# Layer 0's second branch: queries with keys, and values with gates, projected at once, in units of four contraction blocks by 512 columns

## The chip, the core and the metric

The kernel runs on one core of a Trainium2 chip. A time is the device time of one execution in microseconds (us); less is better. The time of a kernel is the median of several runs. Beside that there is one profiled execution, whose span and rows are quoted below. Engines are called TensorE (PE), VectorE (DVE), ScalarE (ACT), GpSimd (POOL) and SyncE (SP), which issues the weight loads.

## What is computed

Two blocks of two layers each run over 512 tokens (256 of a context and 256 of the sequence) with a model width of 1024. The change lies in the first layer of the first block, in its second branch: differential attention over 8 heads, each with two maps of width 64 and values of width 128.

```
bq, bk, bv, bz = columns of h @ w_in            # 1024 columns each, h is 512 x 1024
qh = rmsnorm(bq.reshape(n, 8, 2, 64), q_norm_w)  # over the 64
kh = rmsnorm(bk.reshape(n, 8, 2, 64), k_norm_w)
if not context: qh, kh = apply_axial_rope(qh, rope), apply_axial_rope(kh, rope)
s = q @ k.T / 8;  p = softmax(s);  w = p[map 0] - lam * p[map 1]
y_b = rmsnorm(w @ v) * (1 - lam_init) * silu(bz)
```

Context tokens attend to the context (256 keys), the other tokens to all 512. All is float32.

## The kernel before

**Projections.** Weights come from memory in units of 1 MB (128 partitions by 2048 words), through a ring of two buffers `raw`. ScalarE writes the high part of a unit, rounded to the fp32r type of the matmul, to `wh` (`used`, `convert`, L1750 and L1751: 1280 and then 768 words), and VectorE the rest, `raw - wh`, to `wl` (L2528 and L2530, or L2548 from `used_part`). There are two buffers of each as well, so a unit can be converted as soon as TensorE is through with the unit two places before it. The activations `H` are in two parts too. A product is three matmuls (`mm3`): high by high, high by low, low by high.

**The branch.** `branch_b` exists once for each engine, and each engine runs its own list in order. Heads are taken in four pairs. For layer 0 a pair has 16 slots, one for each kind (q, k, v, z) and token tile of 128 tokens, in the order q0 to q3, k0 to k3, v0 to v3, z0 to z3. In a slot `proj_k` does the projection of a tile onto the pair's 256 columns of the kind: 8 contraction blocks by 3 matmuls of 256 columns, with the tile of `H` stationary. A kind's weights are one unit. Two tiles share a PSUM bank; q, v and z use banks 0 and 1, k banks 7 and 6.

`chunk_b` takes the results in the slot after: for q and k ScalarE squares two tiles from PSUM into `b_qn`, VectorE sums the squares, and after the second pair of tiles it computes one reciprocal root for the kind (`root`, eight small operations and one to add eps) and multiplies PSUM by it into `b_qn`. GpSimd then weights the context tiles (0 and 1) and rotates the others (four half-width products with tables `wtab`, L3468, and an addition). In slots 13 and 15 TensorE transposes the pair's queries and keys into banks 6 and 7, and ScalarE copies them to `b_qt`. v is copied and z goes through tanh on ScalarE; VectorE completes the gate.

**The attention of a pair** runs beside the projections of the next one, planned by `slot_b`. A pair has 8 items j (two heads by four query tiles). Scores of an item are in slot 15, 17, 19, ... (every second slot), its transposes two slots later and its product with the values three slots later. Between them lie, on VectorE, the maximum and its factor (L2887, L2513), on ScalarE two exponentials (TMG<-PS), on VectorE the shares (L2875 and then L2517, writing colS, colC and TMG), which TensorE's transpose waits for. TensorE does not start an item's scores before the exponentials of the item before it are done. VectorE does the shares in the slot after the scores. Four items make an output: factors and products by the gate on VectorE (`b_done_slot`), four transposes on TensorE into bank 6 (`b_out_slot`), copies on ScalarE and VectorE into `YB`.

In VectorE's list a slot is: shares, maximum, output, results of the projection (`chunk_b`), conversion of a unit, factors. The first branch's values (`values_of`) are already projected in half units, four contraction blocks by 512 columns, as are those of the Fourier branch (`pair`).

Of the kernel before, what the change touches and what calls it, by code (L numbers as in the profile page):

```python
# [33 lines left out]
def plan_units():  # L34
# [34 lines left out]
    for l in range(2):  # L69
# [21 lines left out]
        for p in range(4):  # L91
# [130 lines left out]
def program(nc, wpk, xin, memt, vec, tabs, tabs2, rpb, out):  # L222
# [13 lines left out]
    with ctx:  # L236
# [217 lines left out]

        def b_chunk(l, n):
# [177 lines left out]
        def tensor_program(P):  # L633
# [354 lines left out]
            def merge_b(l):  # L988
# [29 lines left out]
                for j in range(8):  # L1018
# [4 lines left out]
                    elif l == 0:  # L1023
                        P.wait_ge(dve_step, ("b_z", l, 3, j))
# [22 lines left out]
            def slot_b(l, n):  # L1047
# [28 lines left out]
                if pj := B_VALUES[l].get(n):  # L1076
                    a, t_, nk = b_tile(l, pj[1])
                    P.wait_ge(act_step, ("b_wt", l, *pj))
                    P.wait_ge(act_step, ("b_v", l, pj[0], 1))
# [6 lines left out]
                    t.then_inc(*pe_step.mark(("b_pv", l, *pj)))  # L1086

            def branch_b(l):
# [18 lines left out]
                for n in range(B_BASE[l]):  # L1107
                    p, kind, t_ = b_chunk(l, n)
                    i, half = divmod(t_, 2)
                    slot_b(l, n)  # L1110
                    if (a := B_QK[l].get(n % B_PER[l])) is not None:
                        for c, x in enumerate("qk"):
# [5 lines left out]
                            free[6 + c] = act_step, ("b_qk", l, p, a)  # L1118
                    b = b_bank(l, kind, i)
                    if half == 0:  # L1120
# [3 lines left out]
                        elif kind == "q":  # L1124
                            if p:
                                P.wait_ge(*((dve_step, ("b_z", l, p - 1, i)) if l == 0 else (act_step, ("b_v", l, p - 1, 1))))
                            else:
                                P.wait_ge(act_step, ("m_gate", l, "a", 6 + b))
                        elif kind == "v":
                            if l == 0 or i:  # L1130
# [5 lines left out]
                        else:  # L1136
                            P.wait_ge(act_step, ("b_v", l, p, i if l == 0 else 0))
                    u = place["b_" + kind, 4 * l + p]
# [599 lines left out]
        def scalar_program(A):  # L1738
# [266 lines left out]
            def merge_b(l):  # L2005
# [13 lines left out]
                used("b_z", 4 * l + 3)  # L2019
# [10 lines left out]
            def slot_b(l, n, chunk=None):  # L2030
# [14 lines left out]
                if chunk is not None:  # L2045
                    chunk_b(l, chunk)
# [10 lines left out]
                if pj := B_VALUES[l].get(n):  # L2057
# [8 lines left out]
                    act(y, bank(5)[:, 128 * i:128 * i + 128], ACT.Copy, ("b_osq", l, *pj))  # L2066

# [24 lines left out]
            def branch_b(l):  # L2092
                t0, N = lay(l)
                for n in range(B_BASE[l]):
                    slot_b(l, n, n - 1 if n else None)
# [8 lines left out]
                    if n and b_chunk(l, n - 1)[2] == 3 and (b_chunk(l, n - 1)[1] != "q" or l == 0):  # L2104
                        used("b_" + b_chunk(l, n - 1)[1], 4 * l + n // B_PER[l] - (n % B_PER[l] == 0))
                    if l and n % B_PER[l] == 4:
                        used("b_q", 4 * l + n // B_PER[l])
# [399 lines left out]
        def vector_program(D):  # L2507
# [327 lines left out]
            def merge_b(l):  # L2835
# [14 lines left out]
                slot_b(l, base, base - 1, ("b_z", 4 * l + 3))  # L2850
# [16 lines left out]
            def slot_b(l, n, chunk=None, unit=()):  # L2867
# [22 lines left out]
                if pg := B_OUT[l].get(n):  # L2890
# [3 lines left out]
                        YB[0][:, heads_, t0:512], ALU.mult, ALU.subtract, *events)  # L2894
                if chunk is not None:
                    chunk_b(l, chunk)
# [4 lines left out]
                if pg := B_DONE[l].get(n):  # L2901
# [5 lines left out]
                    for i in range(4):  # L2907
                        a, t_, nk = b_tile(l, 4 * g + i)
                        stt(b_yt[k][:, i], b_yt[k][:, i], small[:, 40 + i:41 + i], b_z[p % 2][:, t_, a], ALU.mult, ALU.mult, ("b_yo", l, p, g))

# [24 lines left out]
            def branch_b(l):  # L2935
# [9 lines left out]
                for n in range(1, B_BASE[l]):  # L2945
                    p, kind, t_ = b_chunk(l, n - 1)
                    slot_b(l, n, n - 1, ("b_" + kind, 4 * l + p) if t_ == 3 and kind != "q" else ())
                    if l and n % B_PER[l] == 4:
                        used("b_q", 4 * l + p)
                    if l == 0 and n % B_PER[l] in (5, 6):  # L2950
                        used_part("b_q", p, n % B_PER[l] - 5)
# [514 lines left out]
        def pool_program(G):  # L3466
# [24 lines left out]
            def branch_b(l):  # L3491
# [14 lines left out]
                for n in range(1, B_BASE[l] + 1):  # L3506
                    p, kind, t_ = b_chunk(l, n - 1)
                    if kind in "qk" and t_ == 3:
                        c = "qk".index(kind)
                        ones = lambda x, m: x.unsqueeze(1).to_broadcast([128, m, 64])  # L3510
                        if kind == "k" or l == 0:
                            G.wait_ge(dve_step, ("b_norm", l, p, kind, 0))
                            x = b_qn[c][:, 0:2].rearrange("p t (g d) -> p (t g) d", d=64)
                            tt(x, x, ones(b_w[:, c], 8), ALU.mult)
                        G.wait_ge(dve_step, ("b_norm", l, p, kind, 1))
                        G.wait_own(pool_step)
                        for t in range(2):
                            x = b_qn[c][:, 2 + t].rearrange("p (g s d) -> p g s d", g=4, s=2)
                            m2 = b_m2[:, t].rearrange("p (g s d) -> p g s d", g=4, s=2)
                            sines = b_tab[:, c, 1, t].rearrange("p (s d) -> p s d", s=2).unsqueeze(1).to_broadcast([128, 4, 2, 32])  # L3520
                            tt(m2, x[:, :, ::-1], sines, ALU.mult)
                        G.wait_own(pool_step)
                        for t in range(2):
                            x = b_qn[c][:, 2 + t].rearrange("p (g d) -> p g d", d=64)
                            tt(x, x, ones(b_tab[:, c, 0, t], 4), ALU.mult)
                        G.wait_own(pool_step)
# [362 lines left out]
```

## Time and profile before

| | us |
|---|---|
| median of 3 runs | 2238.47 |
| lowest and highest | 2237.56, 2239.45 |
| the profiled execution | 2240.27 |
| its span | 2238.1 |

The span runs from the first to the last instruction in the profile. Busy time is counted per engine and overlaps between engines. Matmuls are pipelined, so their durations overlap one another: what a stream of them costs is read from the distance of their starts, not from their durations. A row `xN` merges N instructions of one kind that follow one another. In the timeline the text in square brackets is the idle time before a row and what ended it.

### The profile page before, as it was taken

How to read it: one execution, taken by the hardware profiler on the slowest of the kernel's cores; microseconds unless marked ns; L12 is line 12 of the kernel's file. 1: busy time of each engine (PE TensorE's matmuls, PEld its weight loads, DVE VectorE, ACT ScalarE, POOL GpSimd, SP SyncE). 2: the span in 40 equal slices, each digit the busy share in tenths (PEclk: the TensorE clock that was granted, in tenths of full speed). 3: DMA queues.
4: the chain of work that ended last, by engine and by line, in shares of the span. 5: the costliest groups of instructions: out<-in, count | busy, mean ns of one | idle time of the engine just before them, and what ended most of it. 6: DMA issues, size and time to landing. Idle time of an engine off the chain costs nothing.

```text
span 2238.1 us, 34826 instructions
## 1 busy us (share of the span) xinstructions
PE 2215.1 (99%) x14398; PEld 1948.8 (87%) x14398; DVE 1350.9 (60%) x2589; ACT 1046.2 (47%) x1994; POOL 273.4 (12%) x298
## 2 busy tenths in 40 slices
PE   8999999999999999999999999999999999999998
PEld 7888878999978888878899999999888888988887
DVE  6644523566755243466465776557777776667875
ACT  5543422345442233354443455445466554466553
POOL 0000000222201032100002220120210110120110
PEclk9999999999999999999999999999999999999999
DMA  8522134221224222235343223446533545324544
GB/s 313 186 94 78 74 151 171 76 77 58 76 97 148 94 76 94 85 132 170 113 151 132 76 95 114 170 170 211 158 110 147 188 169 187 133 95 151 188 173 147
DMA packets 55534, 298.07 MB, mean 133 GB/s; under 512 B 9344, under 2 KB 16256, under 8 KB 24208
## 3 DMA queue, kind: packets, MB, share of 16 engines
q1 hardware_dynamic: 53040, 291.62, 36.4%
q10 hardware_dynamic: 2336, 4.23, 0.8%
q8 instruction: 113, 1.85, 0.3%
q14 instruction: 45, 0.37, 0.1%
HBM read 292.65 MB, written 3.44 MB: 132 GB/s over the span
## 4 chain that ended last, share of the span: by engine, by line
PE 92%; DVE 5%; ACT 2%; DMA 1%; issue 0%; ACTq 0%; POOL 0%; SPq 0%; DVEq 0%
PE PS L637 88%; PE PS L641 4%; DVE TM L2509 1%; ACT TM L1740 1%; DVE wl L2528 1%; ACT TMG L1740 0%; DVE wl L2530 0%; DMA raw<-in_wpk 0%; DVE colS L2517 0%; DMA Y<-factors_d 0%; DVE HY L2517 0%; DVE TM L2678 0%; DVE TMG L2517 0%; ACT wh L1750 0%; ACT HY L1740 0%
## 5 line engine op out<-in xcount | busy, mean ns | idle before, releaser
L637 PE MATMUL PS<-HY,wh 128*128 128x512 f32 (+3 forms) x4944 | 1282.4, 343 | 5.1 <-ACT TM L1740 1.4
L637 PEld LDWEIGHTS PS<-HY,wh 128*128 128x128 f32 (+2 forms) x4944 | 847.9, 189 | 121.5 <-issue 8.5
L637 PE MATMUL PS<-HY,wl 128*128 128x256 f32 (+1 forms) x3000 | 925.0, 308 | 0.0
L637 PEld LDWEIGHTS PS<-HY,wl 128*128 128x128 f32 x3000 | 566.7, 189 | 30.0
L2528 DVE TENSOR_TENSOR wl<-raw,wh 128x1280 fp32r<-128x1280 f32 (+1 forms) x238 | 346.9, 1458 | 387.8 <-ACT wh L1750 387.7
L637 PE MATMUL PS<-wh,HY 128*128 128x256 f32 (+1 forms) x2468 | 527.3, 306 | 0.2
L1740 ACT ACTIVATE TM<-PS 128x512 f32<-128x512 f32 (+3 forms) x399 | 196.7, 508 | 527.9 <-PE PS L637 417.9
L637 PEld LDWEIGHTS PS<-wh,HY 128*128 128x128 f32 x2468 | 405.9, 191 | 19.7 <-ACT TM L1740 0.8
L1750 ACT ACTIVATE wh<-raw 128x1280 fp32r<-128x1280 f32 (+2 forms) x246 | 295.7, 1202 | 245.4 <-PE PS L637 163.5
L637 PE MATMUL PS<-wl,HY 128*128 128x256 f32 (+1 forms) x1234 | 373.4, 303 | 0.0
L2530 DVE TENSOR_TENSOR wl<-raw,wh 128x768 fp32r<-128x768 f32 (+1 forms) x238 | 248.8, 1045 | 0.0
L637 PEld LDWEIGHTS PS<-wl,HY 128*128 128x128 f32 x1234 | 236.1, 191 | 8.6
L1751 ACT ACTIVATE wh<-raw 128x768 fp32r<-128x768 f32 (+2 forms) x246 | 200.2, 814 | 0.0
L637 PE MATMUL PS<-TM 64*128 64x512 f32 (+5 forms) x704 | 134.0, 396 | 1.9 <-ACT TM L1740 1.1
L3468 POOL TENSOR_TENSOR HY<-TM,HY 128x256 fp32r<-128x256 f32 (+2 forms) x64 | 62.7, 980 | 351.2 <-ACT HY L1740 350.2
L1740 ACT ACTIVATE TMG<-PS 128x512 f32<-128x512 f32 (+2 forms) x121 | 51.5, 444 | 105.2 <-PE PS L637 98.0
L637 PEld LDWEIGHTS PS<-TM 64*128 64x128 f32 (+2 forms) x704 | 80.4, 189 | 18.0 <-issue 7.4
L2509 DVE TENSOR_TENSOR TM<-PS,TM 128x512 f32<-128x512 f32 (+3 forms) x92 | 47.7, 547 | 72.4 <-ACT TM L1740 70.2
L1740 ACT ACTIVATE TMG<-PS,colS 128x512 f32<-128x512 f32 (+1 forms) x108 | 63.8, 598 | 54.3 <-DVE colS L2513 54.1
L3468 POOL TENSOR_TENSOR TM<-TM,wtab 128x256 f32<-128x256 f32 x64 | 68.2, 1085 | 75.6 <-DVE colS L2875 69.1
L3468 POOL TENSOR_TENSOR TM<-TM,T 128x512 f32<-128x512 f32 (+2 forms) x30 | 31.0, 1048 | 373.9 <-PE PS L637 189.2
L1740 ACT ACTIVATE HY<-TM 128x256 fp32r<-128x256 f32 (+2 forms) x82 | 42.0, 519 | 60.4 <-POOL TM L3468 31.6
(195 smaller groups left out, 1701.9 us busy)
## 6 DMA issues: line engine op xcount, KB each, us to landing
raw<-in_wpk SPq DMA_DIRECT2D x233, 1024.0 KB, 4.8
raw<-in_wpk SPq DMA_DIRECT2D x32, 704.0 KB, 4.1
TM<-in_wpk SPq DMA_DIRECT2D x6, 1024.0 KB, 16.6
Y<-factors_d ACTq DMA_DIRECT2D x16, 256.0 KB, 5.0
X<-in_xin SPq DMA_DIRECT2D x1, 2048.0 KB, 15.4
Y<-in_wpk SPq DMA_DIRECT2D x2, 1024.0 KB, 20.3
Y<-bias_d SPq DMA_DIRECT2D x4, 512.0 KB, 10.2
raw<-in_wpk SPq DMA_DIRECT2D x3, 512.0 KB, 3.6
```

Of the source, the lines that this page charges most:

```text
L637: return P.x.matmul(o, l, r, start=start, stop=stop)
L641: return P.x.transpose(o, i, ident[0:p, 0:p])
L1740: return A.x.activation(o, i, f, **kw).then_inc(*act_step.mark(*events))
L1750: A.x.activation(wh[:, s, 0:c], raw[:, r, 0:c], ACT.Copy).then_inc(*hi_split.mark((u, 0)))
L1751: A.x.activation(wh[:, s, c:n], raw[:, r, c:n], ACT.Copy).then_inc(*hi_split.mark((u, 1)))
L2509: return D.x.tensor_tensor(o, a, b, op).then_inc(*dve_step.mark(*events))
L2528: D.x.tensor_tensor(wl[:, s, 0:c], raw[:, r, 0:c], wh[:, s, 0:c], ALU.subtract).then_inc(*lo_split.mark((u, 0)))
L2530: D.x.tensor_tensor(wl[:, s, c:n], raw[:, r, c:n], wh[:, s, c:n], ALU.subtract).then_inc(*lo_split.mark(u))
L3468: return G.x.tensor_tensor(o, a, b, op).then_inc(*pool_step.mark(*events))
```

## The change

For layer 0 only, a pair's four units are now two of queries with keys and two of values with gates. Each holds four of the eight contraction blocks, and 256 columns of either kind. The number of units, their size and their places in the list of loads stay.

```diff
+        for p in range(4) if l == 0 else ():
+            qk = [base + 256 * p + 64 * i + d for base in (4112, 5136) for i in range(4) for d in halves]
+            for k0 in (0, 4):
+                add("b_qk", [("w_in", l, qk)], k0=k0, kn=4)
+            for k0 in (0, 4):
+                add("b_vz", [("w_in", l, r(base + 256 * p, base + 256 * p + 256)) for base in (6160, 7184)], k0=k0, kn=4)
```

A slot is a tile and a half of the contraction: 4 blocks by 3 matmuls of 512 columns. The order of the 16 slots, the slots in which a unit ends, and the banks:

```diff
+        B_PARTS = ([("qk", 0, t) for t in (0, 1, 2, 3)] + [("qk", 1, t) for t in (2, 3, 0, 1)]
+                   + [("vz", half, t) for pair in (0, 2) for half in range(2) for t in (pair, pair + 1)])
+        B_UNIT_ENDS = {3: ("b_qk", 0), 7: ("b_qk", 1), 13: ("b_vz", 0), 15: ("b_vz", 1)}
+        b_squares = T[:, 908:1420]
+        def b_part_bank(kind, t):
+            if kind == "qk":
+                return (6, 7, 0, 1)[t]
+            return t % 2
-            return b_value_slot(l, p, 4 * g + 3) + ((8, 4), (3,))[l][g]
+            if l == 0:
+                return b_value_slot(l, p, 4 * g + 3) + (4, 10 if p < 2 else 4)[g]
+            return b_value_slot(l, p, 3) + 3
```

The last lines are `b_out_slot`: the output transposes move from slots 0 and 4 to slots 12 and 10. A tile of q and k now fills a bank. Its results, taken after slots 5 and 7 for two tiles at a time, go another way. ScalarE:

```diff
+            def part_b(n):
...
+                    act(squares_, src[0], ACT.Square, ("b_sq", 0, p, "q", i), scale=0.125)
+                    for c in range(2):
+                        act(dst[c], src[c], ACT.Copy, ("b_copy", 0, p, c, i))
+                    A.wait_own(act_step)
+                    A.wait_ge(dve_step, ("b_sum", 0, p, i, "q"))
+                    act(squares_, dst[1], ACT.Square, ("b_sq", 0, p, "k", i), scale=0.125)
...
+                    act(b_v[p % 2][:, t].rearrange("p a d -> p (a d)"), bank(b)[:, 0:256], ACT.Copy, ("b_v", 0, p, t))
...
+                    act(b_z[p % 2][:, t].rearrange("p a d -> p (a d)"), bank(b)[:, 256:512], ACT.Tanh, ("b_zt", 0, p, t), scale=0.5)
```

VectorE, with one root for both kinds of two tiles, and products from SBUF to SBUF:

```diff
+            def part_b(n):
...
+                    for c, x in enumerate("qk"):
+                        D.wait_ge(act_step, ("b_sq", 0, p, x, i))
+                        D.x.reduce_sum(ss[:, 8 * c:8 * c + 8], wide(b_squares), AX).then_inc(*dve_step.mark(("b_sum", 0, p, i, x)))
+                    root(colS[:, 0:16], colS[:, 16:32], ss, eps=EPS)
+                    D.wait_own(dve_step)
+                    for c, x in enumerate("qk"):
+                        D.wait_ge(act_step, ("b_copy", 0, p, c, i))
+                        y = wide(b_qn[c][:, 2 * i:2 * i + 2].rearrange("p t d -> p (t d)"))
+                        tt(y, y, colS[:, 8 * c:8 * c + 8].unsqueeze(2).to_broadcast([128, 8, 64]), ALU.mult, ("b_norm", 0, p, x, i))
+                if half and kind == "vz":
+                    zt = b_z[p % 2][:, t].rearrange("p a d -> p (a d)")
+                    D.wait_ge(act_step, ("b_zt", 0, p, t))
+                    stt(zt, zt, 1.0, bank(b_part_bank(kind, t))[:, 256:512], ALU.add, ALU.mult, ("b_z", 0, p, t))
```

Where a unit is converted (ScalarE; in VectorE's slot 8 the conversion goes ahead of the results as well):

```diff
+                    ends = b_unit_end(n - 1) if n and l == 0 else None
+                    if ends and n % 16 in (8, 14):
+                        used(*ends)
                     slot_b(l, n, n - 1 if n else None)
...
+                    if ends and n % 16 not in (8, 14):
+                        used(*ends)
```

TensorE, a part of a tile:

```diff
+            def part(p, kind, half, t, end):
+                u, b = place["b_" + kind, 2 * p + half], b_part_bank(kind, t)
+                w, v = weights(u)
...
+                for k in range(4):
+                    split_done(u, k)
+                    P.wait_ge(*h_ready(0)(4 * half + k))
+                    own = slice(128 * t, 128 * t + 128)
+                    x = mm3(bank(b), H[0][:, 4 * half + k, own], H[1][:, 4 * half + k, own], w[:, k], v[:, k],
+                            half == 0 and k == 0, half == 1 and k == 3)
```

GpSimd: the tiles that are rotated (2 and 3) are ready first, so the order of a pair is now rotation of q, rotation of k, weighting of q, weighting of k, where it was weighting and rotation of q, then weighting and rotation of k:

```diff
+                for p in range(4):
+                    if l == 0:
+                        rotated(p, "q")
+                        rotated(p, "k")
+                        weighted(p, "q", ("b_ready", l, p, "q", 1))
+                        weighted(p, "k", ("b_ready", l, p, "k", 1))
+                        continue
```

## Rows read from the trace of the kernel before

**Rows 1.** The page: TensorE's busy time; the chain that ended last, by engine and line.
```profile
PE 2215.1 (99%) x14398; PEld 1948.8 (87%) x14398; DVE 1350.9 (60%) x2589; ACT 1046.2 (47%) x1994; POOL 273.4 (12%) x298
...
PE 92%; DVE 5%; ACT 2%; DMA 1%; issue 0%; ACTq 0%; POOL 0%; SPq 0%; DVEq 0%
PE PS L637 88%; PE PS L641 4%; DVE TM L2509 1%; ACT TM L1740 1%; DVE wl L2528 1%; ACT TMG L1740 0%; DVE wl L2530 0%; DMA raw<-in_wpk 0%; DVE colS L2517 0%; DMA Y<-factors_d 0%; DVE HY L2517 0%; DVE TM L2678 0%; DVE TMG L2517 0%; ACT wh L1750 0%; ACT HY L1740 0%
```

**Rows 2.** Windows of the first and last pair: length, each engine's busy us, clock, DMA.
```profile
379.20:427.50 48.30, 48.30 (x402) 47.83 (x402) 22.73 (x44) 14.96 (x23) 17.35 (x24) 1.00 0.35 125
...
555.54:620.25 64.71, 64.58 (x515) 59.09 (x514) 45.96 (x112) 32.87 (x86) 15.06 (x12) 1.00 0.18 66
```

**Rows 3.** Chain in order of time, slots 8 to 11, third pair: start, us, what.
```profile
522.86 0.61 ACT TM L1740
...
526.09 1.29 DVE TM L2509 x2
527.38 2.11 DVE wl L2528
...
531.74 1.03 ACT TMG L1740 x4
...
534.96 0.44 PE PS L641 x2
```

**Rows 4.** Timeline of TensorE, third pair: start, us, line, operands, shape, count.
```profile
522.65 1.05 PE L637 MATMUL PS<-TM 128*128 128x128 f32 x8
...
527.90 0.28 PE L637 MATMUL PS<-wl,HY 128*128 128x256 f32 x1
...
528.26 0.28 PE L637 MATMUL PS<-wl,HY 128*128 128x256 f32 x1
...
533.71 1.13 PE L637 MATMUL PS<-TM 64*128 64x512 f32 x4
```

**Rows 5.** Timeline of TensorE in the first branch's values.
```profile
190.40 0.39 PE L637 MATMUL PS<-wl,HY 128*128 128x512 f32 x1
...
191.08 0.39 PE L637 MATMUL PS<-wl,HY 128*128 128x512 f32 x1
```

**Rows 6.** Groups by line and form, 379 to 621 us: count, busy us, mean ns.
```profile
L637 PE MATMUL PS<-wh,HY 128*128 128x256 f32 x1024 | 196.1, 287 | 0.0
```

**Rows 7.** Timeline of TensorE in the Fourier branch.
```profile
734.47 0.39 PE L637 MATMUL PS<-wl,HY 128*128 128x512 f32 x1
...
735.17 0.39 PE L637 MATMUL PS<-wl,HY 128*128 128x512 f32 x1
```

**Rows 8.** The page, parts 5 and 6: high part of a unit on ScalarE; weight loads.
```profile
L1750 ACT ACTIVATE wh<-raw 128x1280 fp32r<-128x1280 f32 (+2 forms) x246 | 295.7, 1202 | 245.4 <-PE PS L637 163.5
...
raw<-in_wpk SPq DMA_DIRECT2D x233, 1024.0 KB, 4.8
```

**Rows 9.** Timeline of VectorE, slots 5, 6 and 8 to 10 of the third pair.
```profile
513.61 0.53 DVE L2513 TENSOR_SCALAR colS<-colS 128x2 f32<-128x2 f32 x1
514.05 1.48 DVE L2548 TENSOR_TENSOR wl<-raw,wh 128x1280 fp32r<-128x1280 f32 x1
...
527.29 2.20 DVE L2528 TENSOR_TENSOR wl<-raw,wh 128x1280 fp32r<-128x1280 f32 x1
...
530.83 0.68 DVE L2887 TENSOR_REDUCE colS<-PS 128x2 f32<-128x512 f32 x1
531.54 0.17 DVE L2513 TENSOR_SCALAR colS<-colS 128x2 f32<-128x2 f32 x1
...
533.13 1.25 DVE L2517 SCALAR_TENSOR_TENSOR colC<-colS 128x1 f32<-128x1 f32 x1
```

**Rows 10.** Timeline of GpSimd: third pair of layer 0; one row of layer 1.
```profile
526.86 1.28 POOL L3468 TENSOR_TENSOR TM<-TM,T 128x512 f32<-128x512 f32 x1 [6.79 <-DVE TM L2509]
528.29 4.73 POOL L3468 TENSOR_TENSOR TM<-TM,wtab 128x256 f32<-128x256 f32 x4
533.09 1.28 POOL L3468 TENSOR_TENSOR TM<-TM 128x512 f32<-128x512 f32 x1
...
1233.86 3.28 POOL L3468 TENSOR_TENSOR TM<-TM,wtab 128x256 f32<-128x256 f32 x4 [20.18 <-DVE colS L2875]
```

More of the change, by code:

```diff
@@ L90, in plan_units @@
         merge("a", 10256)
-        for p in range(4):
+        for p in range(4) if l == 0 else ():
[4 more added lines that the diff above has]
+                add("b_vz", [("w_in", l, r(base + 256 * p, base + 256 * p + 256)) for base in (6160, 7184)], k0=k0, kn=4)
+        for p in range(4) if l else ():
             for tag, base in (("b_q", 4112), ("b_k", 5136)):
@@ L1086, in slot_b @@
                     t.then_inc(*pe_step.mark(("b_pv", l, *pj)))
+            def part(p, kind, half, t, end):
+                u, b = place["b_" + kind, 2 * p + half], b_part_bank(kind, t)
+                w, v = weights(u)
+                if half == 0 and kind == "qk":
+                    if b >= 6:
+                        P.wait_ge(*free[b])
+                        free[b] = act_step, ("b_copy", 0, p, 1, 0)
+                    elif p:
+                        P.wait_ge(dve_step, ("b_z", 0, p - 1, t))
+                    else:
+                        P.wait_ge(act_step, ("m_gate", 0, "a", 6 + b))
+                elif half == 0:
+                    P.wait_ge(*((dve_step, ("b_z", 0, p, t - 2)) if t >= 2 else (act_step, ("b_copy", 0, p, 1, 1))))
+                for k in range(4):
[4 more added lines that the diff above has]
+                            half == 0 and k == 0, half == 1 and k == 3)
+                if half or end:
+                    x.then_inc(*projected.mark(*([("b_" + kind, 0, p, t)] if half else []), *([("unit", u)] if end else [])))
             def branch_b(l):
@@ L1107, in branch_b @@
                 for n in range(B_BASE[l]):
-                    p, kind, t_ = b_chunk(l, n)
-                    i, half = divmod(t_, 2)
+                    if l:
+                        p, kind, t_ = b_chunk(l, n)
+                        i, half = divmod(t_, 2)
+                    else:
+                        p, kind, half, t_ = b_part(n)
                     slot_b(l, n)
@@ L1118, in branch_b @@
                             free[6 + c] = act_step, ("b_qk", l, p, a)
+                    if l == 0:
+                        part(p, kind, half, t_, b_unit_end(n))
+                        continue
                     b = b_bank(l, kind, i)
@@ L1136, in branch_b @@
                         else:
[L1137 to L1138 removed]
+                            P.wait_ge(act_step, ("b_v", l, p, 0))
+                    u = place["b_" + kind, p]
                     proj_k(bank(b)[:, 256 * half:256 * half + 256], u, H, h_ready(l), 8, 128 * t_, ("b_" + kind, l, p, t_),
@@ L2894, in slot_b @@
                         YB[0][:, heads_, t0:512], ALU.mult, ALU.subtract, *events)
+                if unit and l == 0 and n % 16 == 8:
+                    used(*unit)
+                    unit = ()
                 if chunk is not None:
-                    chunk_b(l, chunk)
+                    chunk_b(l, chunk) if l else part_b(chunk)
                 if pj and b_turn_slot(l, *pj) == n + 1:
@@ L3505, in branch_b @@
                         tt(b_tab[:, c, 1, t, 32:64], b_cs[:, 1, t, 32:64], w[:, 0:32], ALU.mult)
[L3506 to L3526, printed above, removed]
-                        tt(b_qn[c][:, 2:4], b_qn[c][:, 2:4], b_m2, ALU.add, ("b_ready", l, p, kind, 1))
```

98 lines of the change are left out of this document (83 added, 15 removed).

## The prediction, made before the changed kernel had run

> **What bounds the kernel now.** The page comes first: TensorE is busy 99% of the span, and 92% of the chain that ended last lies on it, 88% on one line [rows 1]. So the change gains what it takes from TensorE's stream and loses what TensorE has to wait for. [...] The chain in order of time shows where the stage is tight even now: it leaves TensorE at 522.86, runs over the keys' norm, the conversion of a weight unit, the maximum of the next scores, the exponential and the shares on VectorE, and comes back to TensorE's transpose only at 534.96 [rows 3]. I therefore follow this place slot by slot. A slot is one of the 16 pieces of projection work in a pair; slot 8 of this pair (the third) begins at 522.65 and its slot 11 at 533.71 [rows 4].
>
> **What the matmuls give.** A slot's projection is 24 matmuls of 256 columns now and 12 of 512 columns then. Three matmuls (high by high, high by low, low by high) start 0.36 us apart as groups of 256 columns [rows 4], so a slot costs 8 x 0.36 = 2.88 us. Groups of 512 columns start 0.68 us apart in the first branch's values, which have the same operand roles [rows 5]: 4 x 0.68 = 2.72 us. The branch has 1024 such matmuls with the high part of the weights [rows 6] and, by the code, half as many with the low part, 1536 in all, that is 64 slots. Gain: 64 x 0.16 = **10.2 us**. The bound on the other side is the Fourier branch, where groups of 512 start 0.70 us apart [rows 7]; its stationary operand takes every other column, the new code takes neighbouring ones, so I take 0.68. At 0.70 the gain would be 64 x 0.08 = 5.1 us. Attention matmuls, transposes and their number stay.
>
> **Edits that cost nothing by themselves.** DMAs: the same 16 units of 1 MB in the same queue, with the small bias transfers after the same places in order; a unit's load is issued after the conversion two units earlier, and that leaves at least five slots, some 17 us, against a landing of 4.8 us [rows 8]. ScalarE gets four copies, two SBUF squares and eight narrow evacuations in place of wide ones, about 3 us more per pair (0.61 us for 512 elements [rows 3]), and has 31.8 us idle in a pair. One root for both kinds and two token tiles, twice a pair, is as many root steps as before. Two units of values and gates are now open together, so three conversions have four slots or two slots of time: two slots are 5.4 us of projection and 6.5 to 8 us with attention, ScalarE needs 1.2 us for the larger part of a conversion [rows 8] and, by its 768 words, 0.8 for the smaller, VectorE 1.5 [rows 9] and 0.9; from its start it is some 3.8 us until VectorE is through. That is hidden, provided both engines are free. The output transposes only change their slots (0.44 us each).
>
> **What becomes late: the slot 8 chain.** VectorE works in order: in slot 8 it does the last shares, the conversion, then the whole norm of token tiles 0 and 1 for queries and keys, and only then the maximum of slot 9's scores. TensorE's next scores, in slot 11, wait for that exponential. Now, from the start of slot 8: square until 0.8 and sum until 1.5, root until 3.4 (so it takes 1.9), the two norms of 1.29 together until 4.7, the conversion until 8.2, maximum and exponential until 10.15 [rows 3, 9]; slot 11 begins at 11.06. Margin 0.9 us, for an exponential that ends at 532.77 and scores that start at 533.71. After the change:
> - Slot 6 now has a full chain as well (square q, sum, square k, sum, root, two norms, where it had one square and one sum). It starts behind slot 5's exponential and holds VectorE until about 3.5 us into slot 7. So slot 7's exponential ends 1.6 us after the start of slot 8 instead of 1.1 before it.
> - ScalarE's conversion follows it: high part at 2.9, low parts 1.5 + 0.9 until 5.2.
> - Sum q 0.7, square k 0.6, sum k 0.7 (a sum of 512 elements as the maximum of 512, 0.68 [rows 9], the square as the 0.61 of [rows 3]): 7.1. Root and norms 3.2: 10.3. Maximum, factor and exponential 2.0 [rows 9]: 12.3.
> - Slot 11 begins at 11.0 (three slots shorter by 0.16, an output transpose in slot 10 longer).
> So TensorE is 1.2 to 1.4 us late without any contention; with a small wait for a late transposed copy, or for the shifted output in slot 12 (its factors are ready about 0.3 to 0.4 late), I take 1.5 us a pair, for the three pairs that have attention beside them.
>
> **Contention of VectorE with GpSimd.** This is the larger term. While GpSimd has an operation running, VectorE's operations on SBUF operands last longer: the larger part of a conversion 2.20 us against 1.48, a two-element factor 0.53 against 0.17, and an operation on a single column 1.25 [rows 9]; the 2.20 and the 1.25 began 0.43 and 0.04 us after a GpSimd operation and got through once it had ended (526.86 + 1.28, 533.09 + 1.28) [rows 10]. GpSimd suffers in turn: its four half-width products take 4.73 us beside conversions and 3.28 us without them [rows 10]. So the operations take turns, whole ones at a time. [...]
>
> In the old order GpSimd did keys' rotation alone after slot 8. In the new one it starts at the end of slot 6's norm and does two rotations on end, 2 x (3.3 + 1.3), then both weightings, 2 x 1.4, and the norms themselves now read and write SBUF (they read PSUM). I interleave them by turns: shares of slot 7's scores lose about 0.8 us to the last products of q; the conversion waits for one addition and one product, 1.6 us more; the root meets the keys' addition, 1.3; the two-element factor meets a weighting, 0.7. That is 4.4 us on the same chain. The exponential comes 5.6 us late where each turn is lost, of which 2.1 us is already taken in slot 10 (the transposed copy is behind the late square on ScalarE). The old trace lost about 1.3 us there in a comparable spot, and turns aren't always lost: 0 is the lower bound, 4.4 the upper, and I take 3.7, near the upper because VectorE's six us of such work fall into a stretch in which GpSimd is almost never idle. Per pair 1.5 + 3.7 = 5.2 us, three pairs: **15.6 us**.
>
> **The first pair.** No attention, slots of 2.72. Norm of slot 6 is done 22.1 us after the branch's start, GpSimd needs 2 x 6.1 + 2 x 1.4 = 15.0 us by its rows with conversions beside it [rows 10] and ends at 37.1; the transposes of slot 13 want it at 35.4 and 35.9. So 1.3 us, 2.7 if the root's small steps also take turns with it; I take **2.3 us**.
>
> **Sum.** -10.2 + 15.6 + 2.3 = +7.7 us. Against the profiled execution, 2240.27 us with a span of 2238.1, that is 2248.0. That execution stands 1.8 us above the median of the runs, 2238.47, and carrying the change to the median gives 2246.2. I forecast **2246**, slower. What a measurement can tell from no change is 0.2%, 4.5 us: 2234.0 to 2242.9.
>
> **Rivals.**
> - *Chains late, little lost in turns.* Gain 10.2, loss 3 x 1.5 + 1.3 = 5.8: 2234.1; with half the turns lost, 3 x 2.2 = 6.6 more: 2240.7. For it: what reads PSUM does not lengthen (the maximum at 530.83 takes 0.68 us with GpSimd at work beside it [rows 9, 10]), so part of the chain is immune. Against: the rows of conversions. Mostly within 0.2%.
> - *All hidden, the gain stands.* This is the other side: if TensorE's matmul stream is the only thing that counts and VectorE catches up before slot 11, 2238.5 - 10.2 = 2228.3. It decides from a slot 8 chain 1.3 us shorter than I reckon, with no turn lost. For it: VectorE's 18.7 idle us in the last pair [rows 2]. Against: the margin of 0.9 us now, with one norm less in front of it.
> - *More is late.* All turns lost and a second place behind it (the factors of slot 12, or slot 13's scores): some 8 us a pair, 3 x 8 + 2.7 - 10.2 = +16.5: 2255. Or 512 columns at 0.70: +5.1 on the forecast, 2251.
> - *The columns don't matter.* If groups of 512 took as long as two of 256 (0.72), the gain is 0 and only the delays remain, 2256. The rows of the first branch speak against it.
>
> **Numbers.** Forecast case (2243 to 2251) 0.46; little lost 0.31; all hidden 0.13; more late, with the columns, 0.10. Of the second case 0.04 lies below 2234.0 and 0.02 above 2242.9. Faster 0.04 + 0.13 = 0.17, same 0.25, slower 0.02 + 0.46 + 0.10 = 0.58. The range of 8 in 10 is 2233 to 2253: it leaves out the hidden case and the worst of the last.
>
> **What would show it.** Right: 768 projection matmuls of 512 columns in groups 0.68 apart; idle time of TensorE in slots 10 and 11 of pairs 2 to 4, released by ScalarE's exponential or transposed copy; the last of the chain over colC, colS and wl on VectorE, pairs longer than 64.7 us by 2 to 3; some wait for GpSimd in the first pair's slot 13; conversions of slot 8 longer than 1.5 us. Wrong: pairs of 62 us with TensorE never idle (turns and chains hidden), or idle time released by DMA or by an unfinished conversion, which I price at nothing.

## The result, and the profile after

The changed kernel takes 2260.22 us (median of 4 runs, 2258.51 to 2262.21), the kernel before beside it 2238.56: 1.0097 times as long, with a 95% interval of 1.0084 to 1.011. The prediction had 2246 and a range that ended at 2253: the direction was right, the size was not. The profiled execution took 2262.21 us, with a span of 2260.1.

The page after: TensorE has 768 matmul records fewer than in [rows 1] and the same busy time. Its part of the chain that ended last fell from 92% to 88%, and VectorE's rose to 7%.

```profile
PE 2215.4 (98%) x13630; PEld 1909.8 (84%) x13630; DVE 1356.2 (60%) x2597; ACT 1057.2 (47%) x2026; POOL 267.3 (12%) x298
...
PE 88%; DVE 7%; ACT 3%; DMA 1%; issue 1%; ACTq 0%; POOL 0%; SPq 0%; DVEq 0%
```

The windows of the branch after (from and to, length, busy us and instructions of TensorE, its weight loads, VectorE, ScalarE and GpSimd, granted clock as a share of full speed, DMA share, GB/s). In [rows 2] TensorE covered the first pair (48.3 us) and the last (64.7 us) at a clock of 1.00. Now it is busy for 2.13 of the 8 us from 380 us on, and there and at 420 us the mean clock falls. In windows of 2 us it is 0.50 from 384 to 388 us, 0.53 to 390 and 1.00 from there on; behind the second wait it is 0.50 from 424 to 426 us, 0.65 to 428 and then 1.00. By "the lower level" the 0.50 is meant. The pairs 2 to 4 take 67.2 to 68.3 us.

```profile
380.00:388.00 8.00, 2.13 (x5) 1.75 (x6) 2.95 (x5) 2.00 (x2) 2.04 (x9) 0.69 0.63 245
388.00:396.00 8.00, 8.00 (x32) 6.46 (x32) 0.00 (x0) 0.00 (x0) 0.81 (x4) 0.88 0.17 69
...
420.00:428.00 8.00, 5.56 (x20) 4.12 (x19) 3.30 (x7) 0.66 (x2) 4.07 (x3) 0.79 0.00 0
438.00:505.20 67.20, 63.46 (x311) 47.58 (x310) 43.01 (x101) 34.40 (x90) 13.38 (x12) 0.97 0.21 72
505.20:573.20 68.00, 64.63 (x321) 48.72 (x320) 46.30 (x114) 35.63 (x94) 13.32 (x12) 0.97 0.18 62
573.20:641.50 68.30, 64.77 (x321) 48.52 (x320) 46.23 (x114) 35.62 (x94) 13.37 (x12) 0.98 0.18 62
```

TensorE's timeline after has eight waits over 0.3 us in the branch; the kernel before had none between 379 and 648 us. These are the first four (start, us, line, operation, and in brackets the idle time and what ended it); the third and fourth pair repeat the last two with 0.51 and 2.85, 1.31 and 2.22 us. Behind the first two the next groups of 512 columns start 1.28 us apart (386.46 and 387.74, 424.29 and 425.57), and scores that took 1.13 us in [rows 4] take 2.08.

```profile
385.87 0.79 PE L673 MATMUL PS<-wh,HY 128*128 128x512 f32 x1 [6.59 <-DVE T L2626]
386.46 0.63 PE L673 MATMUL PS<-wl,HY 128*128 128x512 f32 x1
...
387.74 0.63 PE L673 MATMUL PS<-wl,HY 128*128 128x512 f32 x1
...
423.13 0.50 PE L673 MATMUL PS<-wh,HY 128*128 128x512 f32 x1 [2.44 <-DVE TM L2623]
...
424.29 0.63 PE L673 MATMUL PS<-wl,HY 128*128 128x512 f32 x1
...
425.57 0.63 PE L673 MATMUL PS<-wl,HY 128*128 128x512 f32 x1
...
476.53 0.71 PE L673 MATMUL PS<-TM 128*128 128x128 f32 x4 [1.49 <-ACT TM L1805]
...
482.23 2.08 PE L673 MATMUL PS<-TM 64*128 64x512 f32 x4 [2.26 <-ACT TMG L1805]
```

The first wait read back, in the chain in order of time (start, us, what): the load of a weight unit, its conversion on ScalarE and VectorE, and behind that in VectorE's queue the copy of the rotary and weight tables out of bank 6. Slot 0 now writes to bank 6. In the kernel before it wrote to bank 0, and the same copy at 385.12 us held up nobody: slot 0 had begun at 379.21.

```profile
376.82 4.71 DMA raw<-in_wpk
...
381.56 1.28 ACT wh L1815
...
382.86 1.49 DVE wl L2634
384.35 0.87 DVE wl L2636
...
385.28 0.54 DVE T L2626 x2
...
385.87 10.34 PE PS L673 x36
```

The two rows of the kernel before, slot 0's first matmul and the copy:

```profile
379.21 0.39 PE L637 MATMUL PS<-wh,HY 128*128 128x256 f32 x1
...
385.12 0.61 DVE L2520 COPY T<-PS 128x256 f32<-128x256 f32 x2
```

### The profile page after: what moved, and what is told of

The parts are those of the page before. It is cut to its first block, busy times and chain, and to the rows that moved or that the text cites. A ratio compares the mean times of both kernels' runs of the same rounds, so it can differ in the third digit from the quotient of the medians.

```text
span 2260.1 us, 33356 instructions
## 1 busy us (share of the span) xinstructions
PE 2215.4 (98%) x13630; PEld 1909.8 (84%) x13630; DVE 1356.2 (60%) x2597; ACT 1057.2 (47%) x2026; POOL 267.3 (12%) x298
## 3 DMA queue, kind: packets, MB, share of 16 engines
q10 hardware_dynamic: 2336, 4.23, 0.8%
## 4 chain that ended last, share of the span: by engine, by line
PE 88%; DVE 7%; ACT 3%; DMA 1%; issue 1%; ACTq 0%; POOL 0%; SPq 0%; DVEq 0%
PE PS L673 85%; PE PS L677 3%; DVE TM L2615 1%; DVE wl L2634 1%; ACT TMG L1805 1%; ACT TM L1805 1%; DVE colS L2623 1%; DVE wl L2636 1%; DMA raw<-in_wpk 1%; ACT wh L1815 0%; DVE TMG L2623 0%; DVE colC L3029 0%; DVE colS L2993 0%; DMA Y<-factors_d 0%; DVE HY L2623 0%
## 5 line engine op out<-in xcount | busy, mean ns | idle before, releaser
L2634 DVE TENSOR_TENSOR wl<-raw,wh 128x1280 fp32r<-128x1280 f32 (+1 forms) x242 | 351.6, 1453 | 412.6 <-ACT wh L1815 412.4
L673 PE MATMUL PS<-wh,HY 128*128 128x256 f32 (+1 forms) x1956 | 506.8, 343 | 9.2 <-DVE T L2626 6.6
L673 PEld LDWEIGHTS PS<-wh,HY 128*128 128x128 f32 x1956 | 342.0, 192 | 49.4 <-DVE T L2626 6.7
L673 PE MATMUL PS<-wl,HY 128*128 128x256 f32 (+1 forms) x978 | 330.6, 338 | 0.0
L2636 DVE TENSOR_TENSOR wl<-raw,wh 128x768 fp32r<-128x768 f32 (+1 forms) x242 | 254.9, 1053 | 0.0
L673 PEld LDWEIGHTS PS<-wl,HY 128*128 128x128 f32 x978 | 187.5, 192 | 17.6
L3599 POOL TENSOR_TENSOR TM<-TM,wtab 128x256 f32<-128x256 f32 x64 | 62.8, 1002 | 240.8 <-DVE TM L2615 169.0
L2615 DVE TENSOR_TENSOR TM<-TM 128x256 f32<-128x256 f32 (+7 forms) x146 | 65.7, 465 | 6.2 <-POOL TM L3599 1.3
```

What stands on the lines that cost most here:

```text
L673: return P.x.matmul(o, l, r, start=start, stop=stop)
L2615: return D.x.tensor_tensor(o, a, b, op).then_inc(*dve_step.mark(*events))
L2634: D.x.tensor_tensor(wl[:, s, 0:c], raw[:, r, 0:c], wh[:, s, 0:c], ALU.subtract).then_inc(*lo_split.mark((u, 0)))
L2636: D.x.tensor_tensor(wl[:, s, c:n], raw[:, r, c:n], wh[:, s, c:n], ALU.subtract).then_inc(*lo_split.mark(u))
L3599: return G.x.tensor_tensor(o, a, b, op).then_inc(*pool_step.mark(*events))
```

## The measure used below: how far the scores are behind

An attention item's scores are the same matmuls in all kernels, in every second slot. The start of such a matmul, less its start in the kernel before, tells how much a kernel has lost up to there. Two rows of the kernel before, of slots 9 and 13 of the second pair,

```profile
461.81 0.70 PE L637 MATMUL PS<-TM 64*128 64x256 f32 x4
...
476.81 1.13 PE L637 MATMUL PS<-TM 64*128 64x512 f32 x4
```

and those of the changed kernel:

```profile
471.23 0.70 PE L673 MATMUL PS<-TM 64*128 64x256 f32 x4
...
491.57 1.13 PE L673 MATMUL PS<-TM 64*128 64x512 f32 x4
```

Differences of this kind, in us (s9 is slot 9 of a pair; "end" is the first slot behind the fourth pair; the columns are the kernels e1, e7, e2, e12, e8 and e4 of the next section):

| scores, start before | changed | tables moved | wait added to before | GpSimd out | both: tables, GpSimd | idle filled | chain in slot 9 |
|---|---|---|---|---|---|---|---|
| pair 1 s15, 423.46 | 10.55 | 2.06 | 9.53 | 6.24 | -2.44 | 7.08 | 10.15 |
| pair 2 s9, 461.81 | 9.42 | 0.92 | 9.53 | 5.11 | -3.57 | 5.94 | 9.01 |
| pair 2 s13, 476.81 | 14.76 | 5.51 | 9.54 | 6.57 | -2.12 | 10.57 | 14.85 |
| pair 3 s9, 526.51 | 12.54 | 3.29 | 9.53 | 4.35 | -4.34 | 8.35 | 12.64 |
| pair 3 s13, 541.51 | 18.08 | 8.76 | 9.54 | 6.45 | -2.23 | 13.70 | 17.36 |
| pair 4 s9, 591.21 | 15.86 | 6.54 | 9.53 | 4.23 | -4.45 | 11.48 | 15.14 |
| pair 4 s13, 606.21 | 21.58 | 12.22 | 9.54 | 6.62 | -2.05 | 17.03 | 20.05 |
| end, 620.77 | 20.76 | 11.40 | 9.54 | 5.81 | -2.87 | 16.25 | 19.24 |

One thing in these differences is neither gain nor loss. An output's four transposes take TensorE 0.43 us, and five outputs stood between a slot 13 and the next slot 9 (or the end) and stand between slots 9 and 13 now. So 5 x 0.43 = 2.2 us of work has moved from the one kind of stretch to the other. A row of the kernel before, in slot 0 of the third pair; the next transposes start at 491.28:

```profile
490.85 0.60 PE L641 MATMUL PS<-T,TM 128*128 128x128 f32 x4
```

## Experiments

Unless said otherwise an edit is made to the changed kernel (2260.22 us). Every ratio is to the kernel before, run beside it on the same chip. `...` in an edit stands for lines left out.

**The tables in another bank** (e1_tables).

```diff
-  mm(bank(6)[:, 128 * c + 64 * t_:...], rope1[0:64, c, ...
+  mm(bank(4)[:, 128 * c + 64 * t_:...], rope1[0:64, c, ...
-  free[6] = dve_step, ("b_tables", l)
+  if l:
+      free[6] = dve_step, ("b_tables", l)
...
-  cp(b_cs.rearrange("p s t d -> p (s t d)"), bank(6)[:, 0:256])
+  cp(b_cs.rearrange("p s t d -> p (s t d)"), bank(4)[:, 0:256])
...
```

> Layer 0's rotary and weight tables go to bank 4 and no longer to bank 6, so slot 0 of the second branch no longer waits for VectorE's copy of them. Theory (the start wait is a loss of its own, which the prediction missed): the wait of 6.59 us ahead of the first matmul of slot 0 goes, and with it most of the stretch in which the next groups start 1.28 us apart; the time falls by 6.6 + 2 to about 2251.5 us. Rival (the wait is only handed on: the weights of slot 0 or 1, or the banks of slots 2 and 3, which the late conversions hold up as well, are waited for next): the idle time of TensorE between 379 and 396 us stays within 2 us of 6.6, and the time stays at 2258 to 2261.

Measured: 2249.28 us, ratio 1.0043 (1.0027 to 1.0058). The wait is gone and nothing took its place: in the windows from 372 to 396 us TensorE is busy throughout, at a clock of 1.00. By the scores the start was worth 10.55 - 2.06 = 8.5 us, 6.6 of them idle; in the pairs 2 to 4 the kernel then loses nearly what the changed one loses (15.7 us from slot 9 to slot 13 in sum, against 16.6). The medians differ by 10.9 us, of which the branch has 20.76 - 11.40 = 9.4. The theory holds.

**The same wait in the kernel before** (e7_before_wait).

```diff
+ if l == 0:
+     P.wait_ge(dve_step, ("b_tables", l))
  for n in range(B_BASE[l]):
```

> The kernel before with one wait more: TensorE waits for VectorE's copy of layer 0's tables ahead of the first matmul of the second branch, as slot 0 of the changed kernel does. Theory (the wait alone makes the loss at the start, whatever the units' shape): TensorE is idle for some 6.5 us from 379.2, the groups after it run at the lower clock for some us, and the time rises by 8 to 11 us to 2247 to 2250. Rival (before, work later in the pair has slack that takes the wait up, or the clock stays): 2244 or less.

Measured: 2249.84 us, 1.0043 (1.0028 to 1.0058), 9.3 us more than before. TensorE is idle for 6.85 us, the windows behind show a clock of 0.62 and 0.74, and the scores are 9.53 us late at once and stay exactly that late to the end of the branch. So the wait makes this loss with the old units as well, and no slack later on takes it back.

```profile
380.00:388.00 8.00, 1.97 (x9) 1.97 (x10) 2.95 (x5) 2.00 (x2) 1.87 (x8) 0.62 0.59 230
388.00:396.00 8.00, 8.00 (x53) 8.00 (x53) 0.58 (x1) 0.60 (x1) 0.97 (x5) 0.74 0.21 84
396.00:412.00 16.00, 16.00 (x136) 16.00 (x135) 7.24 (x16) 3.09 (x4) 7.14 (x6) 1.00 0.12 44
```

**GpSimd's part left out** (e2_no_gpsimd).

```diff
- rotated(p, "q"); rotated(p, "k"); weighted(p, "q", ...); weighted(p, "k", ...)
...
+ tt(b_qn[c][:, 0, 0:1], b_qn[c][:, 0, 0:1], b_w[:, c, 0:1], ALU.mult, ("b_ready", l, p, x, 1))
```

> GpSimd's rotation and weighting of layer 0's queries and keys is left out but for one element each, so what follows computes with unrotated values. [...] Rival (the order alone: the norm chain put ahead of the results of the slot): the waits stay at 3 us or more a pair and the time stays above 2255.

Measured: 2247.78 us, 1.0039 (1.0026 to 1.0052), where 2244 us was the forecast if the turns with GpSimd make a good part of the loss. The wait at slot 12 of the first pair is gone, and those of the pairs 2 to 4 sum to 1.31, 1.35 and 1.64 us. VectorE's timeline shows why. The root in the changed kernel, first pair, beside GpSimd (GpSimd's rows there: 416.81 for 2.98 us, 419.86 for 1.31), and the shares and the conversion of the second pair:

```profile
416.76 0.17 DVE L2619 TENSOR_SCALAR small<-colC 128x16 f32<-128x16 f32 x1
416.97 0.60 DVE L2620 TENSOR_SCALAR colS<-small 128x16 int32<-128x16 int32 x1
417.61 0.66 DVE L2615 TENSOR_TENSOR colS<-colS 128x16 f32<-128x16 f32 x1
...
420.06 1.35 DVE L2623 SCALAR_TENSOR_TENSOR colS<-colS 128x16 f32<-128x16 f32 x2
...
469.43 1.54 DVE L2623 SCALAR_TENSOR_TENSOR TMG<-TMG,colS 128x256 f32<-128x256 f32 x1
470.89 2.02 DVE L2634 TENSOR_TENSOR wl<-raw,wh 128x1280 fp32r<-128x1280 f32 x1
472.83 1.49 DVE L2636 TENSOR_TENSOR wl<-raw,wh 128x768 fp32r<-128x768 f32 x1
```

and the same instructions without GpSimd:

```profile
415.94 0.17 DVE L2619 TENSOR_SCALAR small<-colC 128x16 f32<-128x16 f32 x1
416.15 0.17 DVE L2620 TENSOR_SCALAR colS<-small 128x16 int32<-128x16 int32 x1
416.36 0.17 DVE L2615 TENSOR_TENSOR colS<-colS 128x16 f32<-128x16 f32 x1
...
417.40 0.39 DVE L2623 SCALAR_TENSOR_TENSOR colS<-colS 128x16 f32<-128x16 f32 x2
...
464.60 0.49 DVE L2623 SCALAR_TENSOR_TENSOR TMG<-TMG,colS 128x256 f32<-128x256 f32 x1
465.24 1.49 DVE L2634 TENSOR_TENSOR wl<-raw,wh 128x1280 fp32r<-128x1280 f32 x1 [0.15 <-ACT wh L1815]
466.64 0.95 DVE L2636 TENSOR_TENSOR wl<-raw,wh 128x768 fp32r<-128x768 f32 x1
```

The four products of GpSimd's row at 416.81 end at 417.55, 418.24, 419.09 and 419.78, and the four root steps that take 0.60 to 0.67 us there end at 417.57, 418.27, 419.12 and 419.82. That, and the 0.17 us of each without GpSimd, is what "turns" stands for.

**Its control, and both cures together** (e11_before_no_gpsimd: the same left out of the kernel before; e12_tables_no_gpsimd: e1's and e2's edits together).

> The control: the kernel before with GpSimd's rotation and weighting of layer 0's queries and keys left out but for one element each (what follows computes with unrotated values). In the kernel before TensorE had no wait over 0.3 us between 379 and 648 us, so by the theory (GpSimd's turns cost time only where VectorE's queue has no slack) nothing comes of it: 2236 to 2240 us. Rival (GpSimd's work costs the second branch time in either kernel, so the gain of the changed kernel without it says nothing about the change): 2232 or less.

> The changed kernel with the tables in bank 4 and without GpSimd's rotation and weighting of layer 0 (the same part left out). Theory: the start's loss (9.5 to 11 us) and the turns' loss (12.4 us alone, the wait at slot 12 with it) stand by themselves, so 2260.2 - 11 - 12.4 = 2237 us; against the control the columns' gain of 10 to 11 us less what VectorE's order alone costs in the pairs 2 to 4 (6 us by the offsets of the scores' starts) leaves -4 us or so. Rival (the two losses share a part): 2240 or more.

Measured: the control 2238.7 us, 1.0 (0.999 to 1.0009): GpSimd's turns cost the kernel before next to nothing (0.59 us at the end of the branch). Both cures 2237.67 us, 0.9992 (0.9982 to 1.0001), where the sum of the two gave 2237: the losses stand by themselves. Against the control that is only 1.0 us less, not 4; the scores at the end of the branch say 2.3 less (-2.87 against -0.59).

The kernel with both cures shows the columns' gain and the order's price without the other terms. In the first pair the groups of 512 columns start 0.68 us apart; in the pairs 2 to 4, with attention between them, 0.69. A slot's projection lasts 2.82 to 2.95 us there until the next operation starts, and 2.95 to 3.05 in the kernel before, where groups of 256 are 0.36 apart throughout. Two rows of the third pair, one group apart:

```profile
493.24 0.39 PE L673 MATMUL PS<-wl,HY 128*128 128x512 f32 x1
...
493.93 0.39 PE L673 MATMUL PS<-wl,HY 128*128 128x512 f32 x1
```

TensorE waits 4.3 us in sum in the pairs 2 to 4: 1.9 for the exponential (slot 11), 0.8 for the factored outputs and 1.6 for the gate of the first tile (both slot 12). The third pair:

```profile
530.02 1.13 PE L673 MATMUL PS<-TM 64*128 64x512 f32 x4 [0.39 <-ACT TMG L1806]
...
534.68 0.66 PE L677 MATMUL PS<-T,TM 128*128 128x128 f32 x4 [0.41 <-DVE TM L2624]
...
536.34 0.50 PE L673 MATMUL PS<-wh,HY 128*128 128x512 f32 x1 [0.56 <-DVE TM L2624]
```

**Idle time filled** (e3_keep, e8_keep_sized; n small matmuls behind a wait for results that are there by then).

```diff
+ if l == 0:
+     keep(50, 5)                       # e8: keep(28, 5)
+ if p and n % 16 in (10, 11) or n == 12:
+     P.wait_ge(act_step, ("b_copy", 0, p, 1, 0))
+     keep({10: 9, 11: 17, 12: 16}[n % 16], 7)     # e8: {10: 5, 11: 10, 12: 10}
```

> Small matmuls (128 columns, results that nobody reads) fill TensorE's idle stretches: 50 ahead of slot 0, 16 at slot 12 of the first pair, 9 and 17 at slots 10 and 11 of the pairs 2 to 4. Theory (what the waits cost beyond their own length is the clock: after each idle stretch the groups run at the lower level for some us): the same waits end at the same times, the groups after them start 0.68 us apart in place of 1.28, and the time falls by 6 to 10 us to about 2250 to 2254. Rival (the clock follows something else, or the small matmuls cost as much as they give): 2258 to 2264.

> The small matmuls of the kernel that filled TensorE's idle stretches, but as many as the waits hold (each took 0.229 us, two passes of 128 columns: 50 of them filled 11.43 us where the wait was 6.59): 28 ahead of slot 0, 10 at slot 12 of the first pair, 5 and 10 at slots 10 and 11 of the pairs 2 to 4. Theory (the clock costs 2 us or more at each of five places): the first real matmul of slot 0 starts at 386 as in the changed kernel, the groups after it are 0.68 us apart at once, and the time falls by 6 to 9 us to 2251 to 2254. Rival (the clock gives nothing back, later waits grow by what is won): 2258 to 2262.

Measured: e3 2266.44 us, 1.0114 (1.0098 to 1.013). It tells little: its 50 small matmuls (100 instructions in the trace) took 11.43 us where the wait was 6.59, so slot 0 began at 390.20. e8 2256.23 us, 1.0071 (1.0056 to 1.0086): 4.0 less where 6 to 9 were expected. The clock is 1.00 in all windows of the branch, in both kernels, where the changed kernel has 0.69 and 0.79, so it is behind idle time that it falls. But most of the gain is in the first pair, 10.55 - 7.08 = 3.5 us. In the pairs 2 to 4 the scores lose 15.5 us from slot 9 to slot 13 in sum, against 16.6 with the low clock. Slot 11's scores come as late after slot 9's as in the changed kernel (11.0 us in the second pair of both). Behind them TensorE, at the full clock, has to wait in slot 12 for the factored outputs or the gate, 0.5 to 1.0 us a pair, which it does not where it is slower. So the 2 us or more that I expected at each place are not to be had in these pairs.

**The chain in another place.** Pieces of VectorE's queue in slots 8 to 10 were moved in three ways, two of them also with the tables in bank 4.

e4_split: ScalarE's square of the keys, and VectorE's sum of it, root and norms, one slot later, behind the maximum of slot 9's scores.

```diff
+ late = n % 16 == 8        # e9: (9 if p else 8)
- if half and kind == "qk" and t % 2:
+ if late or half and kind == "qk" and t % 2:
...
+         if i == 0 and late != (x == "k"):
+             continue
...
```

> The norm chain of a pair's first tile is taken apart from the results of slot 8: the square of the keys on ScalarE and the sum of the keys, the root and the norms on VectorE come one slot later, behind the maximum of slot 9's scores. Theory (order: the chain put ahead of the maximum and of the weights' conversion makes slots 10 and 11 wait): the waits at slots 10 and 11 shrink by about 2 us a pair, with about 2 us of clock a pair, so 2248 us; the first pair is as before. Rival (VectorE's queue has no slack there, so the same work one slot later makes slot 12 or 13 late instead): waits of about the same sum at later slots and a time within 3 us of 2260.

Measured: 2260.22 us, 1.0093 (1.0077 to 1.0109): no change. Slot 10 and the scores of slot 11 are in time, and slot 11's transposes wait instead, for shares that now stand behind the chain and take turns with GpSimd (1.38 us where 0.49 would do).

```profile
479.70 1.03 DVE L2630 SCALAR_TENSOR_TENSOR colS<-colS,small 128x1 f32<-128x1 f32 x1
...
480.83 1.38 DVE L2630 SCALAR_TENSOR_TENSOR TMG<-TMG,colS 128x256 f32<-128x256 f32 x1
```

```profile
482.26 0.69 PE L677 MATMUL PS<-T,TMG 128*128 128x128 f32 x2 [3.35 <-DVE TMG L2630]
```

e9_late_root: sum, root and norms once more later, behind those shares; e10_tables_root: that with the tables in bank 4.

> The norm chain of a pair's first tile split once more for the pairs 2 to 4: the sum of the keys' squares, the root and the norms come on VectorE only in slot 10, behind the weights of slot 9's scores, which the slot 11 waited for (3.0 to 3.35 us) when the chain came in slot 9; the first pair as in that kernel. Theory (VectorE's order decides, and the chain itself has slack until GpSimd's work for slot 13): no wait over 1 us at slots 10 and 11, GpSimd's work of the first tile ends in time for slot 13, and the time falls by 3 x (3.4 + 1.5) to about 2245 us. Rival (VectorE and GpSimd have no slack left in a pair, wherever the chain stands): the wait comes back at slots 12 to 14 with 2.5 us a pair or more, and the time stays above 2255.

> The same together with the tables in bank 4. If both theories hold, 2260 - 11 - 15 = 2234 us, under the kernel before (2238.5); if the late root gives nothing, 2249.

Measured: 2264.24 us, 1.0108 (1.0092 to 1.0123), and 2254.59 us, 1.0068 (1.0055 to 1.0082). TensorE now waits 4.14 to 4.66 us a pair in slot 12 for the factored outputs, the next thing in the queue.

e5_late_conv: the conversion of slot 8 to the end of slot 9; e6_both: that with the tables in bank 4.

```diff
  if unit and l == 0 and n % 16 == 8:
-     used(*unit)
      unit = ()
+ if l == 0 and n < B_BASE[l] and n % 16 == 9:
+     unit = b_unit_end(n - 2)
```

> VectorE's conversion of the weight unit freed after slot 7 (3.4 us, two subtractions) is moved from the head of slot 8, ahead of the norm chain of the pair's first tile, to the end of slot 9, behind that chain and behind the maximum of slot 9's scores; ScalarE's half of the conversion stays. Theory (order: the chain is late because the conversion stands ahead of it, and the maximum and ScalarE's square are late behind it): the waits at slots 10 and 11 of the pairs 2 to 4 (3.4 to 3.75 us a pair) fall to under 1 us a pair with their clock loss, and the conversion is still in time for slot 12; about 2260 - 3 x 5 = 2245 us; the first pair keeps its wait of 2.4 us at slot 12. Rival (GpSimd's turns: the earlier chain now runs beside more of GpSimd's work and takes as much longer, or the conversion becomes the thing that slot 12 waits for): the waits of a pair stay over 2.5 us in sum, perhaps at slot 12, and the time stays above 2254.

> The tables in bank 4 (11 us less alone) and the late conversion together. If the two losses stand by themselves and both edits work, 2260 - 11 - 15 = 2234 us, under the kernel before by 4 to 5 us; if the late conversion gives nothing, 2249.

Measured: 2273.21 us, 1.0145 (1.0128 to 1.0162), and 2263.64 us, 1.0105 (1.009 to 1.012). The conversion was due in slot 10 already, not in slot 12 as I had read the ring of two: TensorE waits for it there, 8.27 us in the first pair and 4.75 to 5.02 in the others. With each of the three placements the rival holds: the wait only moves. That VectorE has no room from slot 8's results to slot 13 is read from this. It is not idle for long there: in the second pair of the changed kernel 0.76 us for a square of ScalarE and 1.09, 1.09 and 1.20 us for exponentials, each time for the input of its next operation.

## Why the prediction came out too low

The losses and gains, from the table of the scores:

| term | predicted | measured | from |
|---|---|---|---|
| columns | -10.2 | -8.0 | e12: -8.83 in the 52 slots without waits, less 2.2 of moved transposes: -6.65; 12 more slots of 0.11 |
| wait at slot 0 | none | +8.5 | 10.55 - 2.06 |
| slot 12, first pair | +2.3, at slot 13 | +4.5 | 2.06 + 2.44 |
| turns with GpSimd, pairs 2 to 4 | 3 x 3.7 = 11.1 | +10.6 | 16.60 - 5.96, slots 9 to 13 |
| order alone, pairs 2 to 4 | 3 x 1.5 = 4.5 | +5.1 | e12: 5.96, less the 2.2 of transposes, and 12 slots of 0.11 |
| sum | +7.7 | +20.7 | at the end of the branch +20.76 |

**What the matmuls give: right in kind, a fifth too much.** The 768 matmuls are there (512 with the weights' high part, 256 with the low). But the 0.68 us of the first branch holds only for the first pair, where e12 gains 2.44 us in 15 slots, 0.16 a slot. With attention between the slots the groups are 0.69 apart and the gain is 0.11 a slot: 8.0 us in all, between the forecast 10.2 and its bound of 5.1.

**The step that failed: "Edits that cost nothing by themselves".** It follows DMAs, conversions and copies and leaves out which bank a slot writes to. The diff has it, `(6, 7, 0, 1)[t]`, and `free[6]` was the tables' copy, queued on VectorE behind a conversion whose load lands at 381.5. The trace before shows both, the copy at 385.12 and slot 0 at 379.21. So the wait was put at nothing, without a reason given. Its price is 8.5 us, two thirds of the 13 that the sum lacks. The wait added to the kernel before shows the mechanism by itself; the moved tables show that it can be had back.

**"The first pair": right in kind, wrong in place and size.** GpSimd and VectorE do take turns over the root there (4.7 us from 416.76, where it takes 1.9 without GpSimd). What was late is not GpSimd's end at slot 13 but the gate of the first tile at slot 12, queued behind the norms: 2.44 us idle, and about 2 more until the groups ran at 0.68 us again.

**"What becomes late: the slot 8 chain" and the contention: right.** Waits in slots 10 and 11, released by ScalarE's copy and exponential, in all three pairs. The turns cost 3.5 us a pair, at most 0.4 of it the lower clock, where 3.7 was taken and the bounds were 0 and 4.4. The rows of e2 agree with whole operations taking turns: without GpSimd's work the shares take 0.49 us in place of 1.54 and a root step 0.17 in place of 0.66. What the two engines share was not shown. The order alone was 1.7 a pair against 1.5. The exponential has 0.6 a pair of it in idle time; most of the rest is in slot 12, at the outputs that the prediction had late by 0.3 to 0.4 (0.4 measured) and at the gate, which it did not have.

**Not in the prediction at all: the clock.** After 6.59 and 2.44 us of idling the groups start 1.28 us apart, at a clock of 0.50, up to about 390 us and into the window from 426 to 428 us. That is about 1.9 us in the 8.5 and 2.1 in the 4.5 (idle time taken off). In the pairs it costs next to nothing (1.1 us in sum by the filled kernel).

**The rivals.** "More is late" had 2255 from a second late place in each pair. The time lies above even that, but from the start of the branch. "All hidden" is refuted. "Little lost in turns" is, too, by the 10.6 us, and "the columns don't matter" by the 8.0. The version with both cures, at 2237.67, keeps 2.9 of these 8.0 us; the order takes the rest.

**Open.** No version tried beats the kernel before by more than the noise. What the order costs was not taken away by any edit. Two were not tried: squares of the keys in a buffer of their own, so that ScalarE need not wait for VectorE's sum of the queries' squares (VectorE idles 0.76 us for it in slot 8's chain), and other places for the outputs of slots 10 and 12 than these. The branch accounts for 20.76 of the 21.7 us between the medians. In the profiled execution a place in layer 1 near 1045 us, which the change does not touch, adds 2.6 us: TensorE waits 2.49 us there (before 1.40), and the window from 1045 to 1053 us has a clock of 0.79. Before 2000 us 1.9 of it are made good. In the twelve other kernels the same stretch made between -0.2 and 2.2 us, so I take it for a part of the spread of the runs (2258.51 to 2262.21); it was not tested.

## What to carry to other kernels

When a diff changes the order in which buffers or banks are first used, look up for each first use what last released it, and where that release stands in its engine's queue in the old trace; a late but harmless release becomes the critical one. Price an engine that looks idle on average by the stretch between two results: here VectorE, busy for 68% of a pair, had no room from slot 8 to slot 12, and three reorderings only moved the wait. A gain of 0.11 to 0.16 us a slot is worth taking only if no wait is added, for one wait of 6.6 us cost 8.5, more than all 64 slots gave. And read the matmuls' distance where they will stand, not in another branch.

## What the runs showed of the hardware

- TensorE's granted clock fell to its lower level (0.50 in windows of 2 us) behind idle stretches. 6.59 us idle at the start gave 0.69 and then 0.88 in the two windows of 8 us from 380 us on, 6.85 us in the kernel before with the wait added 0.62 and 0.74; 2.44 us gave 0.79. It did not fall behind every stretch of this kind: it stayed at 1.00 behind 2.41 us in the first pair of e9, 2.23 us in the second pair of e1 and 3.00 us in the third pair of e4. With waits of 0.81 us at most (GpSimd out, pairs 2 to 4) it stayed at 1.00, and with small matmuls in the gaps (e3, e8) too.
- At the lower level groups of 512 columns start 1.28 us apart in place of 0.68 (386.46 and 387.74 us in the changed kernel), and scores take 2.08 us in place of 1.13 (482.23 us).
- The turns lengthened VectorE's smallest operations most in proportion: a factor of one element per partition 1.03 us (e4) in place of 0.22 (e2), a root step 0.66 (changed kernel) in place of 0.17 (e2); a conversion 2.02 in place of 1.49 (the same two).
- Groups of 512 columns start 0.68 us apart in the first pair of e12 and 0.69 in its pairs 2 to 4, where attention stands between the slots; groups of 256 start 0.36 apart throughout the kernel before.
